# Held filters of a long convolution: which half is transformed in the combining stage, and which is stored decayed and transformed in the convolutions

## The reference, cut to what matters

```python
def hyena_filters(L, w1, b1, w2, b2, w3, freq):
    ...
    h = (h @ w3.astype(f32)).reshape(L, HYENA_ORDER, 2, HYENA_WIDTH)
    ...
    decay = jnp.exp(-t * deltas[None, :])
    return h * decay[:, None, None, :]

def fftconv(u, k, bias):
    L = u.shape[1]
    U = jnp.fft.rfft(u, n=2 * L, axis=1)
    K = jnp.fft.rfft(k, axis=0)
    y = jnp.fft.irfft(U * K[None], n=2 * L, axis=1)[:, :L]
    return y + u * bias.astype(jnp.float32)

# in second_block
    z = v.astype(f32)
    for n, gate in enumerate((x1, x2)):
        k = bidir_kernel(filt[:, n, 0], filt[:, n, 1])
        z = gate.astype(f32) * fftconv(z, k, filt_bias[l, n])
```

## Time and profile before

| | us |
|---|---|
| median of 3 runs | 3972.33 (3965.97 to 3974.43) |
| profiled execution | 3975.74, its span 3973.5 |
| TensorE matmul busy | 3715.7 (94%) |
| VectorE busy | 2843.8 (72%) |
| ScalarE busy | 1857.7 (47%) |
| GpSimd busy | 262.9 (7%) |

### The profile page before, as it was taken

The page is one execution under the profiler, slowest core; times in us unless marked ns, Lnnn a source line. Parts: engine busy times, 40 slices in busy tenths (PEclk is TensorE's granted clock), DMA queues, the critical chain, the costliest instruction groups (busy, mean ns, idle before and its releaser), DMA issues. The chain is left out here.

```text
span 3973.5 us, 42171 instructions
## 1 busy us (share of the span) xinstructions
PE 3715.7 (94%) x16780; PEld 2858.1 (72%) x16780; DVE 2843.8 (72%) x2581; ACT 1857.7 (47%) x1719; POOL 262.9 (7%) x281
## 2 busy tenths in 40 slices
PE   8989989799999799999999997899499999999998
PEld 3557766688888677777787533577388888888886
DVE  2655445889888665556245699954698888898887
ACT  3243431677787334443011111110277777777776
POOL 0000000100000200000000000000000101011100
PEclk9999999899999899999999998999799999999999
DMA  3003024899998632223244533143599999999998
GB/s 118 6 15 112 22 74 164 321 418 412 418 415 343 238 115 67 69 75 106 80 122 143 201 133 110 53 159 117 185 368 387 385 389 382 387 381 389 387 382 319
DMA packets 367169, 891.04 MB, mean 224 GB/s; under 512 B 21995, under 2 KB 118610, under 8 KB 357557
## 3 DMA queue, kind: packets, MB, share of 16 engines
q1 hardware_dynamic: 323796, 758.12, 51.3%
q0 software_dynamic: 26896, 97.17, 7.0%
q10 hardware_dynamic: 16336, 33.82, 2.2%
HBM read 788.65 MB, written 100.40 MB: 224 GB/s over the span
## 5 line engine op out<-in xcount | busy, mean ns | idle before, releaser
L2342 DVE TENSOR_TENSOR moe_w_rest<-moe_w_w,moe_upper 128x2048 fp32r<-128x2048 f32 x384 | 862.5, 2288 | 132.6 <-ACT moe_upper L2251 70.2
L2243 ACT ACTIVATE moe_upper<-moe_w_w 128x2048 fp32r<-128x2048 f32 x192 | 357.4, 1909 | 224.8 <-PE moe_y_ps L2207 112.5
L2342 DVE TENSOR_TENSOR moe_w_rest<-moe_w_w,moe_upper_w 128x2048 fp32r<-128x2048 f32 x192 | 430.7, 2286 | 10.5 <-ACT moe_upper_w L2261 10.4
L2261 ACT ACTIVATE moe_upper_w<-moe_w_w 128x2048 fp32r<-128x2048 f32 x192 | 357.5, 1910 | 112.4 <-PE moe_up_ps L2181 79.2
L2251 ACT ACTIVATE moe_upper<-moe_w_w 128x2048 fp32r<-128x2048 f32 x192 | 356.7, 1911 | 1.0 <-DMA moe_w_w<-in_expert_w_dram 0.6
L2181 PE MATMUL moe_up_ps<-moe_upper,moe_x_upper 128*128 128x512 f32 x768 | 308.6, 402 | 0.0
L2181 PE MATMUL moe_gate_ps<-moe_upper,moe_x_upper 128*128 128x512 f32 x768 | 300.8, 392 | 4.7 <-DVE moe_x_rest L2355 4.7
L2181 PE MATMUL moe_gate_ps<-moe_upper,moe_x_rest 128*128 128x512 f32 x768 | 300.6, 391 | 0.0
L2181 PE MATMUL moe_gate_ps<-moe_w_rest,moe_x_upper 128*128 128x512 f32 x768 | 300.3, 391 | 0.0
L2181 PE MATMUL moe_up_ps<-moe_upper,moe_x_rest 128*128 128x512 f32 x768 | 300.1, 391 | 0.0
L2181 PE MATMUL moe_up_ps<-moe_w_rest,moe_x_upper 128*128 128x512 f32 x768 | 299.1, 389 | 0.0
(11 more groups left out here) (616 smaller groups left out, 7649.2 us busy)
## 6 DMA issues: line engine op xcount, KB each, us to landing
moe_w_w<-in_expert_w_dram SPq DMA_DIRECT2D x96, 2048.0 KB, 10.9
moe_w_w<-in_w_gate_dram SPq DMA_DIRECT2D x64, 2048.0 KB, 10.7
moe_w_w<-in_w_up_dram SPq DMA_DIRECT2D x64, 2048.0 KB, 10.4
moe_w_w<-in_w_down_dram SPq DMA_DIRECT2D x64, 2048.0 KB, 10.3
tmp_y_rows<-moe_y ACTq DMA_DIRECT2D x32, 512.0 KB, 8.8
block_w_first<-in_w_in_dram SPq DMA_DIRECT2D x20, 512.0 KB, 3.8
tmp_h<-out_xn POOLq DMA_DIRECT2D x16, 512.0 KB, 3.0
tmp_spectra<-held_K ACTq DMA_DIRECT2D x8, 1024.0 KB, 5.0
```

The costliest lines, as they stand in the source:

```text
L2243: act.activation(half(upper1(c), h), half(weights.w1[c % 2], h), ACT.Copy).then_inc(m.w1_rounded, 1)
L2261: act.activation(half(upper2(i, c), h), half(weights.w2[c % 2], h), ACT.Copy).then_inc(m.w2_rounded, 1)
L2342: dve.tensor_tensor(half(rest, h), half(whole, h), half(upper, h).bitcast(F32), ALU.subtract).then_inc(done, 1)
```

## The change

Of the held half only the blocks of order 0 (units 0, 1, 4, 5: `UNITS`) are transformed, copied, worked by butterflies and stored in the combining stage. The blocks of order 1 (`KEPT`) are made and decayed as before, and stored as they are, 2 MB each, in `filters[2]`. In the convolutions pass 2 gets K steps as passes 1 and 3 have, with `filt` reloaded for passes 2 and 3. The reload stands ahead of the last chunk of U(1, 1) and of U(2, 1) in SyncE's queue. `load_k` is left for pass 0 alone. The core of the diff:

```diff
@@ combine_phase, VectorE
-                if t:
+                if t - 1 in held.UNITS:
                     held.butterflies(c, t - 1)
...
-            held.butterflies(c, NT - 1)
@@ combine_phase, ScalarE
+                if t and t - 1 in held.KEPT_AT:
+                    held.store_filters(act, (t - 1) // HF)
...
-                    held.store(act, t - 2)
+                    if t - 2 in held.UNITS:
+                        held.store(act, t - 2)
...
-                held.copy(act, t, range(len(ahead_of_roots), RADIX))
-            held.store(act, NT - 2)
+                if t in held.UNITS:
+                    held.copy(act, t, range(len(ahead_of_roots), RADIX))
...
-            held.store(act, NT - 1)
@@ combine_phase, TensorE
-                held.transform(pe, t)
+                if t in held.UNITS:
+                    held.transform(pe, t)
@@ FilterSpectra
+    UNITS = [u for u in range(HF * HY_ORDER * 2) if u // HF % HY_ORDER == 0]
+    KEPT = [b for b in range(HY_ORDER * 2) if b % HY_ORDER]
+    KEPT_AT = [HF * b for b in KEPT]
@@ decay_filters
-            dve.wait_ge(m.fwd_made, RADIX * HF * b)
+            dve.wait_ge(m.fwd_made, m.transformed(b - 1))
+        if b - 1 in m.KEPT:
+            dve.wait_ge(m.filt_stored, 16 * (m.KEPT.index(b - 1) + 1))
...
+    def store_filters(m, act, b):
+        s = m.BLOCKS[b][1]
+        act.wait_ge(m.end_set, b + 1)
+        rows = "p d j r c -> p (d j r) c"
+        act.dma_start(m.filters.rearrange(rows)[:, :, bass.ts(s, m.HS)], m.filt[:, :, :, :, :].rearrange(rows)).then_inc(m.filt_stored, 16)
@@ hyena_phase, program
-               ("I", 1, 0), ("U", 2, 1), ...
+               ("K", 2, 0), ("K", 2, 1), ("I", 1, 0), ("U", 2, 1), ...
@@ hyena_phase, SyncE
+        def reload_filters(n):
+            if n in MADE:
+                for b in range(2):
+                    sp.wait_ge(tab.filt_stored[b], 16 * (NT // 2))
+            sp.wait_ge(fwd_made, k_made(n - 1, HF - 1))
+            sp.dma_start(filt[:, :, :, :, :], tab.filters[n]).then_inc(filt_loaded, 16)
...
+                if fh and n + 1 in STORED and i == RADIX - 1:
+                    reload_filters(n + 1)
                 sp.dma_start(u[v % N_CHUNKS][:, :, :], residues(z1 if o else v_x1, RESIDUE[i], h)).then_inc(u_loaded[v % N_CHUNKS], 16)
...
-                elif n not in MADE:
-                    sp.wait_ge(product_ready, HF * (n - 1) + fh + 1)
-                    tab.load_k(sp, K, n, fh)
...
-                if (n, fh) == (2, 0):
-                    for b in range(2):
-                        sp.wait_ge(tab.filt_stored[b], 16 * (NT // 2))
-                    sp.wait_ge(fwd_made, k_made(MADE[0], HF - 1))
-                    sp.dma_start(filt[:, :, :, :, :], tab.filters).then_inc(filt_loaded, 16)
@@ hyena_phase, VectorE, butterflies
-            if n in MADE:
+            if n:
                 dve.wait_ge(fwd_copied, k_made(n, fh))
                 filter_butterflies(c, k)
```

More of the change, by code:

```diff
@@ L3870, with __init__ @@
     BLOCKS = [(o, s) for s in range(2) for o in range(HY_ORDER)]
-    def __init__(self, nc, inputs, spectra):
+    UNITS = [u for u in range(HF * HY_ORDER * 2) if u // HF % HY_ORDER == 0]
+    KEPT = [b for b in range(HY_ORDER * 2) if b % HY_ORDER]
+    KEPT_AT = [HF * b for b in KEPT]
+    def __init__(self, nc, inputs, spectra, filters):
         super().__init__(nc, "held")
-        self.inputs, self.spectra = inputs, spectra
+        self.inputs, self.spectra, self.filters = inputs, spectra, filters
     def __enter__(m):
@@ L3891, in __enter__, with transformed @@
         m.stored = [m.sem(f"stored{b}") for b in range(m.N_K)]
+        m.filt_stored = m.sem("filt_stored")
         return m
+    def transformed(m, b):
+        return RADIX * sum(u // HF <= b for u in m.UNITS)
     def load_second_decay(m, sp):
@@ L3938, in transform @@
         for i in range(RADIX):
-            q = RADIX * u + i
+            q = RADIX * m.UNITS.index(u) + i
             if q >= 2:
@@ L3950, in copy @@
     def copy(m, act, u, groups):
-        b = u % m.N_K
-        if u >= m.N_K:
-            act.wait_ge(m.stored[b], 16 * (u // m.N_K))
+        nth = m.UNITS.index(u)
+        b = nth % m.N_K
+        if nth >= m.N_K:
+            act.wait_ge(m.stored[b], 16 * (nth // m.N_K))
         for i in groups:
-            q = RADIX * u + i
+            q = RADIX * nth + i
             act.wait_ge(m.fwd_made, q + 1)
@@ L3960, in butterflies @@
     def butterflies(m, c, u):
-        c.engine.wait_ge(m.fwd_copied, RADIX * (u + 1))
-        filter_butterflies(c, m.K[u % m.N_K])
+        nth = m.UNITS.index(u)
+        c.engine.wait_ge(m.fwd_copied, RADIX * (nth + 1))
+        filter_butterflies(c, m.K[nth % m.N_K])
         c.engine.sem_inc(m.ready, 1)
@@ L3966, in store @@
         o, s = m.BLOCKS[u // HF]
-        b = u % m.N_K
-        act.wait_ge(m.ready, u + 1)
+        nth = m.UNITS.index(u)
+        b = nth % m.N_K
+        act.wait_ge(m.ready, nth + 1)
         act.dma_start(m.spectra[o, u % HF][:, :, :, bass.ts(s, m.HS)], m.K[b][:, :, :, :]).then_inc(m.stored[b], 16)
@@ L3972, in wait_stored @@
         for b in range(m.N_K):
-            act.wait_ge(m.stored[b], 16 * len(range(b, HF * len(m.BLOCKS), m.N_K)))
+            act.wait_ge(m.stored[b], 16 * len(range(b, len(m.UNITS), m.N_K)))
+        act.wait_ge(m.filt_stored, 16 * len(m.KEPT))
 N_CHUNKS = 3
@@ L3979 @@
 MADE_HALF, = {PASSES[n][1] for n in MADE}
+STORED = range(2, len(PASSES))
 FILTER_STEPS = [(nth, t) for t in range(NT) for nth in range(len(MADE))]
@@ L4121, in store_filter @@
             act.wait_ge(m.filt_ready, s + 1)
-            act.dma_start(m.filters[:, :, t // RADIX, t % RADIX, :], kept).then_inc(m.filt_stored[t % 2], 16)
+            act.dma_start(m.filters[MADE[nth]][:, :, t // RADIX, t % RADIX, :], kept).then_inc(m.filt_stored[t % 2], 16)
     def load_rows(m, sp, v_x1, b):
@@ L4442, in butterflies @@
             back_to(3)
-            if n not in MADE:
-                dve.wait_ge(tab.k_loaded[fh], 16 * (n // HF + 1))
+            if not n:
+                dve.wait_ge(tab.k_loaded[fh], 16)
             for s in range(2):
@@ L4650, in build_program @@
     hidden, spectra = dram("hidden", [FILT_HID, T]), dram("spectra", [HY_ORDER, HF, P, RADIX, 2, HC])
-    filters = dram("filters", [P, 2, HJ, RADIX, HC])
+    filters = {n: dram(f"filters{n}", [P, 2, HJ, RADIX, HC]) for n in STORED}
     ident = nc.alloc_sbuf_tensor("ident", [P, P], F32)
@@ L4713, in build_program @@
         overflow_phase(nc, block, over_done, a["expert_w1"], a["expert_w3"], a["expert_w2"], tables, h2, y_rows, ident, held_in)
-        with FilterSpectra(nc, held_in, spectra) as held:
+        with FilterSpectra(nc, held_in, spectra, filters[STORED[0]]) as held:
             combined = combine_phase(nc, block, over_done, x1, y_rows, tables, a["final_norm_g"], a["g_mix_2"], ident, x2, h_T, held, ahead,
```

6 lines of the change are left out of this document (3 added, 3 removed).

## The result

| | kernel before | changed kernel |
|---|---|---|
| median, 7 runs each | 3967.91 (3965.97 to 3974.43) | 3981.19 (3977.42 to 3984.96) |
| profiled execution | 3975.74, span 3973.5 | 3979.73, span 3978.1 |
| TensorE matmul busy | 3715.7 (94%) | 3709.1 (93%) |
| VectorE busy | 2843.8 (72%) | 2840.8 (71%) |

The ratio of the runs is 1.0029, 95% interval 1.0020 to 1.0039: the changed kernel is slower by some 11.5 us (8 to 15.5). Forecast were 16.7 us more.

A forecast was written before the change was run, and what follows sets the result against it. It took an engine-to-engine chain per row tile to pace the combining stage and VectorE to bound the convolutions. -12.1 + 28.8 = +16.7 us on a median of 3972.33 gave 3989.0, range 3970 to 4001.

The forecast's parts named there:

- Part 1: Combining stage: fewer transforms, copies, butterflies and stores there; 12.1 us less, bounds 8 and 17.
- steps a and c: Combining stage: add(5) starts 5.9 us earlier, x(5) load allowed 4.5; lead stays 5.4 us to decay_filters(3)'s end.
- Step b: Start of decay_filters(2): 0.5 us charged for TensorE's low clock; the wait for stored filters costs nothing.
- Step d: Tail behind decay_filters(3): VectorE's queue takes 15.7 us instead of 25.1; next stage starts 14.8 us earlier.
- Step e: Start of the next stage: TensorE at the low clock after about 10 us idle; 2.7 us taken back.
- Step g: U(1, 1)'s last chunk behind the 4 MB reload lands after 14.7 us; TensorE stands still 7.9 us.
- Step h: Convolutions: U(1, 1) 2.5 us late, added K(2, 0), K(2, 1); first result of I(1) 18.3 us later, filter_butterflies(2, 0) free.
- Step i: Behind I(1)'s first result: filter_butterflies(2, 1) cost 7.5 us, U(2, 1) held up by the second reload 3.0 us.
- part 2: Convolutions: added K steps, butterflies and reloads; 18.3 + 7.5 + 3.0 = 28.8 us more, bounds 15.1 and 37.
- Rival A: Convolutions: chunks not held up, only VectorE's 15.1 us paid; net +3.0, 3975 us; chance 12%.
- Rival B: Combining stage is TensorE's, four transforms worth 45 us; net -16, 3956 us; chance 13% including a milder form, 3968.
- Rival C: Stores and loads collide: part 1 gives 6 or less, reloads land after 19 us; net up to +31; chance 13%.

The follow-up runs named there:

- the second profile: The unmodified changed kernel run and profiled once more, beside the kernel before on the same chip; median 3981.37 us, ratio 1.0029 to before.
- ten profiles: Profiles of the changed kernel and variants with its order of VectorE's work in the combining stage; that stage takes 130.5 to 132.0 us.
- part2_only: Kernel before with only the convolutions changed, pass 2's spectra made from pass 3's stored filters; median 3993.77 us, ratio 1.0060 to before.
- part1_only: Changed combining stage with the convolutions of the kernel before, held loads reading the first convolution's spectrum; median 3954.41 us, ratio 0.9959 to before.
- late_reload: Changed kernel with each 4 MB reload directly behind the last chunk of U(n, 1), not ahead; median 3982.24 us, ratio 1.0027 to before.
- no_bfly_20: Changed kernel without VectorE's filter butterflies of (2, 0); median 3981.14 us, ratio 1.0033 to the kernel before.
- no_bfly_21: Changed kernel without VectorE's filter butterflies of (2, 1); median 3981.13 us, ratio 1.0026 to the kernel before.
- on_pool_2: early_reload with the filter butterflies of (2, 0) and (2, 1) on GpSimd instead of VectorE; median 3980.46 us, ratio 1.0025 to before.
- early_reload: Changed kernel with each 4 MB reload issued ahead of SyncE's wait for the last chunk's free buffer; median 3971.68 us, ratio 1.0002 to before.
- reordered: early_reload with spectrum stores behind the second norm's root and combining-stage butterflies moved to later places; median 3967.91 us, ratio 0.9995 to before.

## Why the prediction came out as it did

It was right in direction, by its own mechanism, and 5.2 us too high in size (16.7 against 11.5). Each part alone, by the runs, gave 16 us off where the sum had 12.1, and 24 us on where it had 28.8. Step by step:

- **Part 1, steps a and c: right in kind, a little too generous.** add(5) came 3.6 us earlier than before (counted from the filters' first matmul), 5.5 in the second profile, where I had 5.9: the load of x(5) took 7.0 and 5.3 us and not the 4.5 that I allowed. The bare clock flatters the forecast here: add(5) at 1368.74 and the next stage at 1428.16 look like the 1368.9 and 1428.8 of the sum, but 2.4 us of that were won ahead of the stage. The lead at the end of decay_filters(3) was 3.3 us where I had 5.4.
- **Step b: the 0.5 us for the low clock was too little** in six of ten profiles (12.31 against 10.63 us for unit 4; part2_only, with the old stage, has 12.22 as well), and the new wait of VectorE for the stored filters cost nothing, as said: no row of VectorE waits for it.
- **Step d held.** From decay_filters(3)'s end to the next stage's first matmul: 15.4 us by the trace (1412.77 to 1428.16), 15.7 by the sum, 25.1 before.
- **Step e, 2.7 us, was mis-sized.** TensorE did begin at the low clock behind 10.10 us of idle time (the turn of tile 7 took 1.97 us), but nothing of it shows in the stretch up to U(0, 0): 786.4 to 787.5 us in the ten profiles above, 788.01 in before and 786.55 in part2_only, which both have the old combining stage. The stage itself gave 13.0 us against before and 14.2 from part2_only to part1_only (145.33 and 131.15), where step d had 14.8.
- **Step g held almost to the number**: landing 14.5 us by the trace, 14.7 by the sum; stop of TensorE 8.05 against 7.9. The 14.7 was a choice between 13.1 and 19.0, so its closeness is in part luck. The Trainium skill (DMA: Bandwidth & Descriptors, "Queues, rings and completion order") says that descriptors of one ring start in order; the trace agrees with it, the chunk landing 1.4 us after the 4 MB ahead of it (0.38 us between the issues, and 1.0 us more to landing), and late_reload agrees from the other side.
- **Step h, 18.3 us: 16.3** against before's profile, 18.0 against part1_only's (198.16 and 180.13). VectorE waited 1.57 us for U(1, 1) and not 2.5. Filter_butterflies(2, 0) lay in the wait and cost nothing, as said (no_bfly_20).
- **Step i, 7.5 + 3.0: the sum held better than its names.** Butterflies(2, 1) began 25.7 us later than before (2461.67 and 2452.52, each from its U(0, 0)), against 28.8. But the 7.5 us are no cost of their own: without them the time is the same (no_bfly_21). By the forecast's own numbers U(2, 1) was ready at 2481.3 and the butterflies done at 2478.3, so TensorE's chain set the time and I could have read that off. "VectorE bounds the convolutions" was true of before and not of the changed kernel, where two chains run 2 us apart.
- **The end of part 2**: 22.1 and not 25.7, since before's profiled execution had the low clock in I(3). A stall of 3.4 us that comes and goes belongs into the bounds of a sum made against one profiled execution.

Rival A was the nearest in size: some 15 us are what part 2 costs in the traces once the reload goes out earlier, but only half of them are VectorE's. What spoke for it, that landing is not bound to the order of issue, no run showed. Rival B fell with part1_only. Rival C was seen in small: the load of x(5) took 4.7 to 7.2 us in every profile with the stored filters and not 3.3, yet part 1 kept its gain.

Open: whether the 2 MB store of filters is what slows the load of x(5), and what decides whether TensorE's clock falls in an idle time of some 3 us.

## What to carry to other kernels

When a large load is added, ask what is issued behind it, on its own queue and on the others, and when that is needed; issue it as soon as its own buffer is free, ahead of the queue's other waits. Here the place of one line was worth 9.7 us, about as much as the change had cost in all. And when work is added to the engine that bounds, check which chain bounds afterwards: if the sum shows two that end within a few microseconds, no single one of them carries the price. Last, a profiled execution is one draw: when it lies well above the median, look for stalls that come and go before putting their time into a sum.

## What the runs showed of the hardware

- GpSimd and VectorE slow each other on elementwise work in SBUF. GpSimd's sum of 128x1024 took 2.3 to 3.8 us against VectorE's 1.23 (in on_pool_2, 2.39 where VectorE stood still and up to 3.80 beside it), and VectorE's own instructions of two tensors took up to 4.88 us for 0.69 beside it. The Trainium skill (SBUF — State Buffer, "SBUF: two separate sides") says that the two engines share one pair of ports as an exclusive lock, held for a whole instruction, and that a VectorE instruction with two SBUF inputs contends for it with a GpSimd instruction that reads SBUF. The trace agrees: VectorE's 128x512 took 4.88 us while GpSimd had a 128x2048 of 5.37 us.
- The 4 MB load took 12.4 and 12.5 us in early_reload (no chunk close to it), 13.5 and 13.2 in the changed kernel (three chunks issued within 7 us behind it), 15.9 and 14.1 in late_reload (a chunk and a store of z, 1 MB, issued within 1.5 us ahead of it, more chunks behind).
- 512 KB issued within 0.4 us behind the 4 MB took 14.5 us (14.2 the second time) on SyncE's queue and 14.0 on GpSimd's; just ahead of the 4 MB they took 5.9 and 6.1 (4.8 and 3.8 the second time).
- TensorE's clock behind the same short idle time in I(3) differs between profiles: by the records' durations it was low behind 2.48, 2.56, 3.06 and 3.12 us, high behind 3.19 to 3.42, and in reordered high for the first group behind 3.63 us and then low. Longer idle times do not go with the low level here. From the first of these groups to the merge it was 34.5 us with the low level (before) and 31.2 without (changed kernel).
